# Inverses of a chunked recurrence on TensorE: the transposed half kept with exchanged partition halves, X and T products issued together

## The chip, the cores and the metric

One NeuronCore of one Trainium2 chip runs the whole kernel in a single launch. The metric is the time of one execution in device microseconds. Times of single instructions come from one profiled execution of the same program.

## The reference, cut to what matters

The reference is two transformer-like blocks over 256 tokens of width 1024, all in float32. The second block has a bidirectional recurrence with 8 heads of 64 columns:

```python
def step(S, inp):
    r_t, w_t, k_t, v_t, kk_t, a_t = inp
    s_kk = jnp.einsum('bhij,bhj->bhi', S, kk_t)
    S = (S * w_t[:, :, None, :]
         - s_kk[..., None] * (a_t * kk_t)[:, :, None, :]
         + v_t[..., None] * k_t[:, :, None, :])
    return S, jnp.einsum('bhij,bhj->bhi', S, r_t)
```

It runs once forward and once backward over the tokens. The kernel computes it in two chunks of 128 tokens. Inside a chunk the term with s_kk makes each token depend on those before it; written out for the chunk this is a triangular system, I + N, for each head and direction. So each chunk needs 16 inverses of 128x128 triangular matrices (8 heads, 2 directions). Ahead of the recurrence stand the first block and the projections, behind it banded attention, output projections and a mixture of 16 experts.

## The kernel before, in words

The kernel is one program in which each engine has its own instruction stream, and semaphores join them. PSUM has eight banks; for each bank two counters exist, `full[b]` (TensorE has finished a filling) and `evac[b]` (some engine has emptied it). The table STAGES lists how often each stage fills each bank; `take` lets PE wait until a bank is empty, `got` lets a reader wait until it is full, and `evacuated` waits until it has been emptied. A filling's place is given by its stage, its bank and its number in that stage.

The loop `for s in range(2)` goes over the two chunks. For each chunk:

- PE makes the score matrices (line 1427) and DVE copies their kept parts into AM (line 2833). ACT takes the two 64x64 diagonal blocks of each into AD (line 2106).
- PE makes the right-hand sides W (lines 1442 and 1446 for the first chunk, 1461 and 1467 for the second); ACT copies them out (line 2118).
- The inverse. The two 64x64 diagonal blocks of every matrix lie in the two partition halves (0 to 63 and 64 to 127). Xw holds the running inverse, XT its transpose, 8 heads in each direction d, 128x512 numbers for a direction. There are N_LEV = 6 levels. A level lv from 1 to 5 does: POOL makes the mask product NL of that level (line 908); PE makes P = NL times Xw (call at line 1493), ACT copies it into Pw (line 2122); PE makes two families, the X products from XT and Pw (call at line 1502) and the T products from Pw and XT (call at line 1504); DVE subtracts them from Xw and XT (line 2856). Level 0 is short: PE transposes NL with an identity (line 1485), DVE subtracts the result from the identity to get Xw (line 2844), and makes XT from NL itself (line 2840, with the semaphore x_init).
- All these products go through the helper `diagonal`, whose matmul is at line 1477. It reads and writes the same partition half, 16 matmuls of 64x64 with 64 columns for a direction. A matmul of float32 leaves two records in the trace, here called passes. P goes to banks 0 and 3, X to banks 1 and 5, T to banks 2 and 6 (direction 0 and 1).
- The blocks off the diagonal: line 1512 (AM and Xw, read out by ACT at line 2127), line 1523 (Pw and XT, read out by ACT at lines 2134 and 2136 into EB), then the inverse is put to W at lines 1534 and 1541, with the gate products (`gate2`, matmuls at line 927) between.

The order of work on PE is the written one: in a level P for direction 0, P for direction 1, then X and T for direction 0, then X and T for direction 1. Each waits with `take` for its bank and with `evacuated` for its operands. ACT takes its copies in the order of P, DVE its updates in the order Xw(0), XT(0), Xw(1), XT(1). SP's queue loads the weights: one part from a ring of four pages, the expert weights when counters such as `ex_started` say that PE has come far enough. No transfer belongs to the inverse.

Of the kernel before, what the change touches and what calls it, by code (L numbers as in the profile page):

```python
# [23 lines left out]
HEADS = 8  # L24
# [20 lines left out]
H = P // 2  # L45
# [43 lines left out]
for _s in range(2):  # L89
    STAGES += [(f"am{_s}", {0: 4, 1: 4, 2: 4, 3: 4}), (f"wv{_s}", {2: 1, 6: 1, **({3: 1, 7: 1} if _s else {})}),  # L90
               (f"inv{_s}", {0: 6, 3: 6, 1: 6, 5: 6, 2: 6, 6: 6}),
               (f"tail{_s}", {0: 1, 5: 1, 1: 1 - _s, 6: 1 - _s, 2: 1, 3: 1, 7: 2})]
# [50 lines left out]

LORA_BANKS = (7, 5, 6)
# [200 lines left out]
def build(nc, dram, out_dram):  # L345
# [8 lines left out]
    with ctx:  # L354
# [292 lines left out]
        x_init = sem("x_init")  # L647
# [195 lines left out]
        def _(pool):  # L843
# [45 lines left out]
            for s in range(2):  # L889
# [9 lines left out]
                for lv in range(1, N_LEV):  # L899
                    for d in range(2):  # L900
                        u8 = slice(8 * d, 8 * d + 8)
                        if lv == 1:

                            got(pool, f"inv{s}", (1, 5)[d], 0)
                            pool.wait_ge(x_init, 2 * s + d + 1)
                        else:
                            got(pool, f"inv{s}", 3 * d, lv - 2)
# [8 lines left out]
        def _(pe):  # L916
# [498 lines left out]
            for s in range(2):  # L1415
# [17 lines left out]
                if s == 0:  # L1433
                    evacuated(pe, "toks", 5, 2)
                    evacuated(pe, "toks", 6, 2)
                    for d in range(2):
                        take(pe, "wv0", 2 + 4 * d, 0)
                    for b in range(4):
                        evacuated(pe, "am0", b, 3)
                    for hd in range(HEADS):  # L1440
                        for d, near in enumerate((lo64, hi64)):
                            mm(ps[2 + 4 * d][near, 64 * hd:64 * hd + 64], lhsT=AM[near, 8 * d + hd, 256 + near.start:256 + near.stop],
                               rhs=Vtok[near, d, 64 * hd:64 * hd + 64], start=True, stop=True)
                    for hd in range(HEADS):
                        for d, far in enumerate((hi64, lo64)):
                            ins = mm(ps[2 + 4 * d][far, 64 * hd:64 * hd + 64], lhsT=AM[:, 8 * d + hd, 256 + far.start:256 + far.stop],
                                     rhs=Vtok[:, d, 64 * hd:64 * hd + 64], start=True, stop=True)
                            if hd == HEADS - 1:
                                ins.then_inc(full[2 + 4 * d], 1)
                else:  # L1450
                    for d in range(2):
                        evacuated(pe, "tail0", (1, 6)[d], 0)
                        for par in range(2):
                            take(pe, "wv1", 2 + 4 * d + par, 0)
                    for b in range(4):
                        evacuated(pe, "am1", b, 3)
                    for j in range(4):
                        for d in range(2):
                            for par in range(2):
                                hd = 2 * j + par  # L1460
                                mm(ps[2 + 4 * d + par][:, 64 * j:64 * j + 64], lhsT=AM[:, 8 * d + hd, 256:384],
                                   rhs=Vtok[:, 1 - d, 64 * hd:64 * hd + 64], start=True, stop=False)
                        for d in range(2):
                            row = 8 * d + 2 * j + 1 - d
                            for par, r64 in enumerate((lo64, hi64)):
                                b = 2 + 4 * d + par
# [5 lines left out]
                def diagonal(out, d, lhs, rhs):  # L1472

                    for hd in range(HEADS):
                        for q_ in range(2):
                            r64 = slice(H * q_, H * q_ + H)
                            ins = mm(out[r64, H * hd:H * hd + H], lhsT=lhs[r64, 8 * d + hd, :],  # L1477
                                     rhs=eye2[r64, :] if rhs is None else rhs[r64, 8 * d + hd, :], start=True, stop=True)
                    return ins

                for d in range(2):
# [3 lines left out]
                    diagonal(ps[bx], d, NL, None).then_inc(full[bx], 1)  # L1485
                for lv in range(1, N_LEV):
                    for d in range(2):
# [40 lines left out]
                for d in range(2):  # L1528
                    for b in (2 + 4 * d, 3 + 4 * d)[:1 + s]:
# [7 lines left out]
                for d in range(2):  # L1537
                    evacuated(pe, f"inv{s}", (2, 6)[d], 5)
# [261 lines left out]
        def _(act):  # L1800
# [296 lines left out]
            for s in range(2):  # L2097
# [10 lines left out]
                for d in range(2):  # L2108
                    if s:
                        got(act, "tail0", 2 + d, 0)  # L2110
                    for par in range(1 + s):
                        b = 2 + 4 * d + par
# [953 lines left out]
```

## Time and profile before

| what | value |
|---|---|
| median of three runs | 2027.17 us |
| lowest and highest | 2021.96, 2028.55 us |
| the profiled execution | 2026.23 us |
| its span, first to last instruction | 2024.3 us |
| mean granted TensorE clock | 0.943 |
| PE busy | 1784.4 us, 88% |
| DVE busy | 815.0 us, 40% |
| ACT busy | 307.4 us, 15% |
| POOL busy | 94.8 us, 5% |
| HBM read | 423.56 MB |

The profile gives for each engine the time in which it had an instruction in work; passes of TensorE overlap, so its busy time counts a stretch once however many run in it. The granted clock is a share of full speed: 1.00 is 2.4 GHz and 0.50 is 1.2 GHz. The chain that ended last goes back from the last instruction, each time to what released it. The page's slices show PE at 90% or more of the time until late in the run, and in the last part the DMA of the expert weights at some 430 GB/s.

### The profile page before, as it was taken

To read this page: it belongs to the slowest core of one execution; us is meant where nothing else is said; L and a number is where in the kernel's file an instruction comes from. 1 tells how busy PE (TensorE), PEld (TensorE's weight loads), DVE (VectorE), ACT (ScalarE), POOL (GpSimd) and SP (SyncE) were. 2 spreads that over 40 slices of the span, in tenths; PEclk is the share of its full clock that TensorE was granted. 3 is DMA by queue.
4 is the path that set the end of the run, shared out by engine and by line. 5 is a ranking of instruction groups with operands and counts; after the bars stand their busy time and mean duration, and the time that the engine had idled before them with its cause. 6 is when DMAs were issued, how large, how long until landed. Compare 5 with 4: busy or idle time off the path is not lost.

```text
span 2024.3 us, 29056 instructions
## 1 busy us (share of the span) xinstructions
PE 1784.4 (88%) x12002; PEld 1372.9 (68%) x12002; DVE 815.0 (40%) x1648; ACT 307.4 (15%) x704; POOL 94.8 (5%) x110
## 2 busy tenths in 40 slices
PE   7999999999999999999999998999997765565655
PEld 2788888888884877669999997878777221121212
DVE  3766666964431130734675247442534010000001
ACT  2200000011210111412111124222322000000000
POOL 2000000010100000000000002311001000000000
PEclk9999999999999999989999999999998877787887
DMA  8333335955441113116545852100467799999996
GB/s 356 127 131 142 126 128 181 350 202 187 146 146 62 63 63 125 63 63 229 186 166 188 291 189 102 44 23 24 145 253 308 331 433 428 433 435 427 432 435 255
DMA packets 46320, 426.10 MB, mean 210 GB/s; under 512 B 5283, under 2 KB 5764, under 8 KB 14988
## 3 DMA queue, kind: packets, MB, share of 16 engines
q1 hardware_dynamic: 36576, 387.04, 49.1%
q10 hardware_dynamic: 9644, 37.59, 5.2%
q8 instruction: 79, 1.29, 0.3%
q14 instruction: 21, 0.17, 0.0%
HBM read 423.56 MB, written 1.05 MB: 210 GB/s over the span
## 4 chain that ended last, share of the span: by engine, by line
PE 31%; DMA 19%; DVE 3%; issue 1%; POOL 1%; ACT 1%; SPq 0%; POOLq 0%; DVEq 0%; ACTq 0%
DMA arena<-experts_ring_dram 19%; PE bank L927 15%; PE bank L1102 6%; PE bank L1477 3%; PE bank L1726 2%; PE bank L1313 1%; DVE arena L2833 1%; PE bank L1580 0%; PE bank L1627 0%; POOL rstd L859 0%; PE bank L1363 0%; PE bank L1687 0%; DVE rstd L2234 0%; POOL arena L908 0%; PE bank L1646 0%
## 5 line engine op out<-in xcount | busy, mean ns | idle before, releaser
L927 PE MATMUL bank<-arena 128*128 128x256 f32 (+2 forms) x3552 | 684.8, 354 | 12.3 <-DVE arena L2739 5.6
L927 PEld LDWEIGHTS bank<-arena 128*128 128x128 f32 x3552 | 582.9, 192 | 104.8 <-issue 33.3
L1726 PE MATMUL bank<-arena 128*32 128x512 f32 x1536 | 237.9, 777 | 166.6 <-DMA arena<-experts_ring_dram 163.8
L1726 PEld LDWEIGHTS bank<-arena 128*32 128x32 f32 x1536 | 64.7, 137 | 334.1 <-issue 331.0
L1051 PE MATMUL bank<-arena 128*128 128x256 f32 x880 | 193.9, 379 | 0.0
L1051 PEld LDWEIGHTS bank<-arena 128*128 128x128 f32 x880 | 167.1, 190 | 23.1 <-issue 0.5
L1102 PE MATMUL bank<-arena 128*128 128x128 f32 x1064 | 119.0, 275 | 0.0
L1102 PEld LDWEIGHTS bank<-arena 128*128 128x128 f32 x1064 | 118.9, 192 | 0.0
L3026 DVE TENSOR_TENSOR arena<-arena,bank 128x512 f32<-128x512 f32 x8 | 5.5, 688 | 251.0 <-PE bank L1726 251.0
L2398 DVE SCALAR_TENSOR_TENSOR arena<-arena 128x1024 f32<-128x1024 f32 x56 | 68.3, 1220 | 0.0
L859 POOL TENSOR_TENSOR rstd<-sq 128x128 f32<-128x128 f32 (+2 forms) x9 | 6.6, 738 | 1258.5 <-ACT sq L1817 1258.5
L1477 PE MATMUL bank<-arena 64*64 64x64 f32 x2048 | 61.0, 218 | 1.1 <-POOL arena L908 1.0
L1477 PEld LDWEIGHTS bank<-arena 64*64 64x64 f32 x2048 | 60.2, 135 | 1.8 <-POOL arena L908 1.7
L3032 DVE COPY arena<-bank 128x512 f32<-128x512 f32 x4 | 2.8, 691 | 143.0 <-PE bank L1726 143.0
L1194 PE MATMUL bank<-arena 128*128 128x256 f32 x256 | 55.6, 379 | 0.0
L1817 ACT ACTIVATE sq<-bank 128x128 f32<-128x128 f32 (+1 forms) x48 | 14.9, 311 | 255.1 <-PE bank L927 224.0
L1194 PEld LDWEIGHTS bank<-arena 128*128 128x128 f32 x256 | 48.6, 190 | 7.0 <-issue 0.5
L2397 DVE SCALAR_TENSOR_TENSOR fh<-arena 128x1024 f32<-128x1024 f32 x36 | 44.0, 1224 | 13.7 <-DMA arena<-ada_rest_dram 11.4
L1313 PE MATMUL bank<-arena 128*128 128x128 f32 x384 | 47.2, 279 | 1.1 <-DVE arena L2266 1.0
L1313 PEld LDWEIGHTS bank<-arena 128*128 128x128 f32 x384 | 44.6, 192 | 3.1 <-DVE arena L2266 2.9
L1875 ACT ACTIVATE arena<-bank 128x256 f32<-128x256 f32 x22 | 8.3, 382 | 227.0 <-PE bank L1051 227.0
L1817 ACT ACTIVATE sq<-arena 128x128 f32<-128x128 f32 (+2 forms) x80 | 29.0, 371 | 86.3 <-DVE arena L2947 47.1
(399 smaller groups left out, 1845.0 us busy)
## 6 DMA issues: line engine op xcount, KB each, us to landing
arena<-dense_dram SPq DMA_DIRECT2D x167, 1024.0 KB, 4.8
arena<-experts_ring_dram SPq DMA_DIRECT2D x41, 4096.0 KB, 26.9
arena<-ada_rest_dram ACTq DMA_DIRECT2D x56, 512.0 KB, 5.3
arena<-experts_dram SPq DMA_DIRECT2D x21, 1024.0 KB, 9.3
arena<-ada_head_dram SPq DMA_DIRECT2D x8, 1024.0 KB, 23.8
arena<-experts_ring_dram SPq DMA_DIRECT2D x2, 2048.0 KB, 25.6
arena<-experts_dram SPq DMA_DIRECT2D x6, 512.0 KB, 11.5
arena<-tokens_dram ACTq DMA_DIRECT2D x1, 2048.0 KB, 20.8
```

Source lines behind the costliest of these rows:

```text
L927: ins = mm(out, lhsT=w, rhs=rhs(k), start=k == 0, stop=k == k_tiles - 1)
L1051: ins = mm(ps[b][:, o:o + T], lhsT=lhs(k), rhs=rhs(k), start=k == 0, stop=k == 3)
L1102: ins = mm(ps[b][:, o:o + P], lhsT=lhs(k), rhs=rhs(k), start=k == 0, stop=k == 3)
L1194: ins = mm(ps[tt][:, 0:256], lhsT=h1[:, k, tt * P:tt * P + P], rhs=ring_wide[slot][:, k, :], start=k == 0, stop=k == KD - 1)
L1313: ins = mm(ps[b][:, o:o + P], lhsT=w, rhs=h[:, k, half * P:half * P + P], start=k == 0, stop=k == KD - 1)
L1477: ins = mm(out[r64, H * hd:H * hd + H], lhsT=lhs[r64, 8 * d + hd, :], rhs=eye2[r64, :] if rhs is None else rhs[r64, 8 * d + hd, :], start= ...
L1726: ins = mm(ps[banks[half]][32 * e:32 * e + 32, :], lhsT=lhs[:, 2 * kp + par, CAP * e:CAP * e + CAP], rhs=slab[e][par][:, half * 512:half * ...
L1817: A(square_slot(r, j, n), src, ACT.Square).then_inc(ready, 1)
L1875: A(in_up[s][:, 0, :], ps[a][:, 0:T], ACT.Copy).then_inc(in_copied, 1)
L2397: stt(scratch[:, :], w, 1.0, cond_wide[:, 0:D], mult, mult, accum_out=ada_acc[:, 2 * t:2 * t + 1])
L2398: stt(w, w, 1.0, cond_wide[:, D:2 * D], mult, mult, accum_out=ada_acc[:, 2 * t + 1:2 * t + 2]).then_inc(ada_used, 1)
L2833: V.copy_predicated(AM[:, 8 * d + hd, :], keep_bits[:, d, :], ps[b][:, :]).then_inc(evac[b], 1)
```

## The change

XT is kept with its partition halves exchanged: what belongs to the upper block lies in partitions 0 to 63, and the other way round. Pw is made the same way, since P is now written to the other half. Then an X product reads one half and writes the other, and a T product reads and writes the exchanged half. PE issues them head by head: two X matmuls, two T matmuls, each of the four on another quarter of the array.

At level 0 XT no longer comes from NL by DVE. PE sends NL through the identity into exchanged halves (two matmuls with 512 columns for a direction, banks 2 and 6), and DVE subtracts that from the identity. POOL waits for this product, as it read NL, before it makes the next mask. The semaphore x_init is gone.

In the last level T has to return to its own halves. PE first sends XT through the identity into bank 2 or 6 (two matmuls with 512 columns), and the T products are added to it there, across halves, with Pw negated by ACT; DVE adds instead of subtracting for Xw, and ACT copies the bank to XT. The fillings of banks 2 and 6 become 7 a chunk, one more.

The right-hand sides W move from banks 2, 6, 3, 7 to 0, 3, 7, 6 (RIGHT_BANKS, at lines 1442 to 1467 and in ACT's copies at line 2118), as the level-0 transfer needs 2 and 6.

The diff, cut to its core (the renaming of W's banks is left out):

```diff
-    STAGES += [(f"am{_s}", {0: 4, 1: 4, 2: 4, 3: 4}), (f"wv{_s}", {2: 1, 6: 1, **({3: 1, 7: 1} if _s else {})}),
-               (f"inv{_s}", {0: 6, 3: 6, 1: 6, 5: 6, 2: 6, 6: 6}),
+    STAGES += [(f"am{_s}", {0: 4, 1: 4, 2: 4, 3: 4}), (f"wv{_s}", {0: 1, 3: 1, **({7: 1, 6: 1} if _s else {})}),
+               (f"inv{_s}", {0: 6, 3: 6, 1: 6, 5: 6, 2: 7, 6: 7}),
                (f"tail{_s}", {0: 1, 5: 1, 1: 1 - _s, 6: 1 - _s, 2: 1, 3: 1, 7: 2})]
...
 
...
                             got(pool, f"inv{s}", (1, 5)[d], 0)
-                            pool.wait_ge(x_init, 2 * s + d + 1)
+                            got(pool, f"inv{s}", (2, 6)[d], 0)
                         else:
                             got(pool, f"inv{s}", 3 * d, lv - 2)
                         nc.gpsimd.tensor_tensor(NL[:, u8, :], AD[:, u8, :],
...
-                def diagonal(out, d, lhs, rhs):
-
-                    for hd in range(HEADS):
-                        for q_ in range(2):
-                            r64 = slice(H * q_, H * q_ + H)
-                            ins = mm(out[r64, H * hd:H * hd + H], lhsT=lhs[r64, 8 * d + hd, :],
-                                     rhs=eye2[r64, :] if rhs is None else rhs[r64, 8 * d + hd, :], start=True, stop=True)
-                    return ins
+                halves = (lo64, hi64)
 
                 for d in range(2):
                     bx = (1, 5)[d]
                     pe.wait_ge(nl_ready, s * 2 * N_LEV + d + 1)
                     take(pe, f"inv{s}", bx, 0)
-                    diagonal(ps[bx], d, NL, None).then_inc(full[bx], 1)
+                    for hd in range(HEADS):
+                        for r64 in halves:
+                            ins = mm(ps[bx][r64, H * hd:H * hd + H], lhsT=NL[r64, 8 * d + hd, :], rhs=eye2[r64, :],
+                                     start=True, stop=True)
+                    ins.then_inc(full[bx], 1)
+                    bt = (2, 6)[d]
+                    take(pe, f"inv{s}", bt, 0)
+                    for q_, r64 in enumerate(halves):
+                        ins = mm(ps[bt][halves[1 - q_], :], lhsT=eye2[r64, :], rhs=NL[r64, 8 * d:8 * d + 8, :], start=True, stop=True)
+                    ins.then_inc(full[bt], 1)
                 for lv in range(1, N_LEV):
+                    last = lv == N_LEV - 1
                     for d in range(2):
                         b = 3 * d
                         pe.wait_ge(nl_ready, s * 2 * N_LEV + lv * 2 + d + 1)
 
                         evacuated(pe, f"inv{s}", (1, 5)[d], lv - 1)
                         take(pe, f"inv{s}", b, lv - 1)
-                        diagonal(ps[b], d, NL, Xw).then_inc(full[b], 1)
+                        for hd in range(HEADS):
+                            for q_, r64 in enumerate(halves):
+                                ins = mm(ps[b][halves[1 - q_], H * hd:H * hd + H], lhsT=NL[r64, 8 * d + hd, :],
+                                         rhs=Xw[r64, 8 * d + hd, :], start=True, stop=True)
+                        ins.then_inc(full[b], 1)
                     for d in range(2):
                         b, bx, bt = 3 * d, (1, 5)[d], (2, 6)[d]
+                        evacuated(pe, f"inv{s}", bt, lv - 1)
+                        take(pe, f"inv{s}", bx, lv)
+                        take(pe, f"inv{s}", bt, lv)
+                        if last:
+                            for q_, r64 in enumerate(halves):
+                                mm(ps[bt][r64, :], lhsT=eye2[halves[1 - q_], :], rhs=XT[halves[1 - q_], 8 * d:8 * d + 8, :],
+                                   start=True, stop=False)
                         evacuated(pe, f"inv{s}", b, lv - 1)
-                        if lv == 1:
-                            pe.wait_ge(x_init, 2 * s + d + 1)
-                        else:
-                            evacuated(pe, f"inv{s}", bt, lv - 2)
-                        take(pe, f"inv{s}", bx, lv)
-                        diagonal(ps[bx], d, XT, Pw).then_inc(full[bx], 1)
-                        take(pe, f"inv{s}", bt, lv - 1)
-                        diagonal(ps[bt], d, Pw, XT).then_inc(full[bt], 1)
+                        for hd in range(HEADS):
+                            c64 = slice(H * hd, H * hd + H)
+                            for q_, r64 in enumerate(halves):
+                                o64 = halves[1 - q_]
+                                ins = mm(ps[bx][r64, c64], lhsT=XT[o64, 8 * d + hd, :], rhs=Pw[o64, 8 * d + hd, :],
+                                         start=True, stop=True)
+                            if hd == HEADS - 1:
+                                ins.then_inc(full[bx], 1)
+                            for q_, r64 in enumerate(halves):
+                                o64 = halves[1 - q_]
+                                ins = mm(ps[bt][r64 if last else o64, c64], lhsT=Pw[o64, 8 * d + hd, :], rhs=XT[o64, 8 * d + hd, :],
+                                         start=not last, stop=not last or hd == HEADS - 1)
+                        ins.then_inc(full[bt], 1)
 
                 for d in range(2):
...
                 for d in range(2):
                     evacuated(pe, f"inv{s}", 3 * d, 5)
-                    evacuated(pe, f"inv{s}", (2, 6)[d], 4)
-                    take(pe, f"inv{s}", (2, 6)[d], 5)
+                    evacuated(pe, f"inv{s}", (2, 6)[d], 5)
+                    take(pe, f"inv{s}", (2, 6)[d], 6)
                 for hd in range(HEADS):
...
                     for d in range(2):
                         got(act, f"inv{s}", 3 * d, use)
-                        A(Pw[:, 8 * d:8 * d + 8, :], ps[3 * d][:, :].rearrange("p (i n) -> p i n", n=H), ACT.Copy)\
-                            .then_inc(evac[3 * d], 1)
+                        A(Pw[:, 8 * d:8 * d + 8, :], ps[3 * d][:, :].rearrange("p (i n) -> p i n", n=H), ACT.Copy,
+                          scale=1.0 if use < N_LEV - 2 else -1.0).then_inc(evac[3 * d], 1)
+                for d in range(2):
+                    bt = (2, 6)[d]
+                    got(act, f"inv{s}", bt, 5)
+                    A(XT[:, 8 * d:8 * d + 8, :], ps[bt][:, :].rearrange("p (i n) -> p i n", n=H), ACT.Copy).then_inc(evac[bt], 1)
                 for d in range(2):
                     far = (slice(H, P), slice(0, H))[d]
                     got(act, f"inv{s}", 3 * d, 5)
...
                         got(act, "tail0", 2 + d, 0)
-                    evacuated(act, f"inv{s}", (2, 6)[d], 4)
+                    evacuated(act, f"inv{s}", (2, 6)[d], 5)
                     A(EB[far, 8 * d:8 * d + 8, :], XT[far, 8 * d:8 * d + 8, :], ACT.Copy)
-                    got(act, f"inv{s}", (2, 6)[d], 5)
+                    got(act, f"inv{s}", (2, 6)[d], 6)
                     A(EB[near, 8 * d:8 * d + 8, :], ps[(2, 6)[d]][near, :].rearrange("p (i n) -> p i n", n=H), ACT.Copy,
...
                 eye8 = eye2.unsqueeze(1).to_broadcast([P, 8, H])
                 for d in range(2):
-                    dve.wait_ge(nl_ready, s * 2 * N_LEV + d + 1)
-                    if s:
-
-                        got(dve, "tail0", 2 + d, 0)
-                    tt_(XT[:, 8 * d:8 * d + 8, :], eye8, NL[:, 8 * d:8 * d + 8, :], sub).then_inc(x_init, 1)
-                for d in range(2):
-                    bx = (1, 5)[d]
-                    got(dve, f"inv{s}", bx, 0)
-                    tt_(Xw[:, 8 * d:8 * d + 8, :], eye8, ps[bx][:, :].rearrange("p (i n) -> p i n", n=H), sub)\
-                        .then_inc(evac[bx], 1)
+                    for dst, b in ((Xw, (1, 5)[d]), (XT, (2, 6)[d])):
+                        got(dve, f"inv{s}", b, 0)
+                        tt_(dst[:, 8 * d:8 * d + 8, :], eye8, ps[b][:, :].rearrange("p (i n) -> p i n", n=H), sub).then_inc(evac[b], 1)
                 for lv in range(1, N_LEV):
                     for d in range(2):
                         bx, bt = (1, 5)[d], (2, 6)[d]
                         evacuated(dve, f"inv{s}", bx, lv - 1)
-                        if lv == 1:
-                            dve.wait_ge(x_init, 2 * s + d + 1)
-                        else:
-                            evacuated(dve, f"inv{s}", bt, lv - 2)
-                        for dst, b, k in ((Xw[:, 8 * d:8 * d + 8, :], bx, lv), (XT[:, 8 * d:8 * d + 8, :], bt, lv - 1)):
-                            got(dve, f"inv{s}", b, k)
-                            tt_(dst, dst, ps[b][:, :].rearrange("p (i n) -> p i n", n=H), sub).then_inc(evac[b], 1)
+                        evacuated(dve, f"inv{s}", bt, lv - 1)
+                        for dst, b in ((Xw[:, 8 * d:8 * d + 8, :], bx), (XT[:, 8 * d:8 * d + 8, :], bt))[:1 if lv == N_LEV - 1 else 2]:
+                            got(dve, f"inv{s}", b, lv)
+                            tt_(dst, dst, ps[b][:, :].rearrange("p (i n) -> p i n", n=H), sub if lv < N_LEV - 1 else add)\
+                                .then_inc(evac[b], 1)
                 got(dve, f"tail{s}", 3, 0)
                 ts_(nU[1], ps[3][:, :].rearrange("p (h n) -> p h n", n=64), -1.0, None, mult).then_inc(evac[3], 1)
                 for d in range(2):
```

## Rows read from the trace of the kernel before

**Rows 1.** The page: the chain that ended last, by engine.
```profile
PE 31%; DMA 19%; DVE 3%; issue 1%; POOL 1%; ACT 1%; SPq 0%; POOLq 0%; DVEq 0%; ACTq 0%
```

**Rows 2.** The chain in order of time, both recurrences: start us, us, what.
```profile
1294.36 2.50 POOL arena L908 x2
...
1296.91 27.28 PE bank L1477 x928
...
1324.35 1.13 PE bank L1512 x31
...
1327.07 1.13 PE bank L1523 x31
...
1328.91 1.15 PE bank L1534 x32
1330.06 3.65 PE bank L927 x16
...
1365.39 27.28 PE bank L1477 x928
...
1395.54 1.55 PE bank L1523 x31
...
1397.91 1.98 PE bank L1534 x32
1399.88 5.13 PE bank L927 x16
```

**Rows 3.** The view of line 1477: durations (min/median/max ns), idle before it, who waited for it.
```profile
L1477 PE MATMUL bank<-arena x2048: 217/218/267, 1293.1 to 1392.5; 64*64 64x64 f32 x187
...
  POOL arena L908: 2.6, 6
...
  DVE arena L2856: 27.5, 20
```

**Rows 4.** Timeline of the first inverse: start us, us, engine, line, operation, [idle before it].
```profile
1293.12 2.08 PE L1477 MATMUL bank<-arena 64*64 64x64 f32 x64
...
1294.32 0.69 DVE L2844 TENSOR_TENSOR arena<-arena,bank 128x512 f32<-128x512 f32 x1
...
1295.68 16.49 PE L1477 MATMUL bank<-arena 64*64 64x64 f32 x548 [0.48 <-POOL arena L908]
...
1302.77 0.60 ACT L2122 ACTIVATE arena<-bank 128x512 f32<-128x512 f32 x1 [4.07 <-PE bank L1477]
...
1308.37 0.60 ACT L2122 ACTIVATE arena<-bank 128x512 f32<-128x512 f32 x1 [4.07 <-PE bank L1477]
```

**Rows 5.** Timeline of line 1541, two column halves of the array.
```profile
1333.74 0.22 PE L1541 MATMUL bank<-arena 128*64 128x64 f32 x1
1333.75 0.22 PE L1541 MATMUL bank<-fh,arena 128*64 128x64 f32 x1
1333.80 0.22 PE L1541 MATMUL bank<-arena 128*64 128x64 f32 x1
```

**Rows 6.** Tiled and untiled products: two timeline rows, one group (busy us, mean ns).
```profile
1279.69 2.00 PE L1427 MATMUL bank<-arena 64*128 64x256 f32 x16
...
1594.89 3.64 PE L1726 MATMUL bank<-arena 128*32 128x512 f32 x32 [2.80 <-DMA arena<-experts_dram]
...
L927 PE MATMUL bank<-arena 128*128 128x512 f32 x128 | 56.2, 592 | 0.0
```

**Rows 7.** Timeline: ten DVE operations of 128x512 in a row.
```profile
1284.61 6.20 DVE L2833 COPY_PREDICATED arena<-arena,bank 128x512 f32<-128x512 uint32 x10
```

**Rows 8.** Stretches behind the inverses: engines' busy us, then granted clock, DMA share, GB/s.
```profile
1324.00:1330.00 6.00, 3.58 (x105) 3.19 (x99) 0.78 (x2) 3.56 (x6) 0.00 (x0) 1.00 0.00 0
...
1395.00:1400.00 5.00, 3.69 (x65) 3.45 (x66) 0.00 (x0) 2.62 (x5) 0.00 (x0) 0.60 0.00 0
```

**Rows 9.** The chain as the expert products begin.
```profile
1574.78 11.29 PE bank L1726 x101
1586.09 18.37 DMA arena<-experts_ring_dram
```

More of the change, by code:

```diff
@@ L141, in gate2_at @@
     return (f"tail{t // 2}", 7, t % 2) if t < 4 else ("gates2", 2 + t % 2, t // 2 - 2)
+RIGHT_BANKS = ((0, 7), (3, 6))
 LORA_BANKS = (7, 5, 6)
@@ L646, in build @@
         am_zero = sem("am_zero")
-        x_init = sem("x_init")
         nl_ready = sem("nl_ready")
@@ L1436, in _ @@
                     for d in range(2):
-                        take(pe, "wv0", 2 + 4 * d, 0)
+                        take(pe, "wv0", RIGHT_BANKS[d][0], 0)
                     for b in range(4):
@@ L1441, in _ @@
                         for d, near in enumerate((lo64, hi64)):
-                            mm(ps[2 + 4 * d][near, 64 * hd:64 * hd + 64], lhsT=AM[near, 8 * d + hd, 256 + near.start:256 + near.stop],
+                            mm(ps[RIGHT_BANKS[d][0]][near, 64 * hd:64 * hd + 64], lhsT=AM[near, 8 * d + hd, 256 + near.start:256 + near.stop],
                                rhs=Vtok[near, d, 64 * hd:64 * hd + 64], start=True, stop=True)
@@ L1445, in _ @@
                         for d, far in enumerate((hi64, lo64)):
-                            ins = mm(ps[2 + 4 * d][far, 64 * hd:64 * hd + 64], lhsT=AM[:, 8 * d + hd, 256 + far.start:256 + far.stop],
+                            ins = mm(ps[RIGHT_BANKS[d][0]][far, 64 * hd:64 * hd + 64], lhsT=AM[:, 8 * d + hd, 256 + far.start:256 + far.stop],
                                      rhs=Vtok[:, d, 64 * hd:64 * hd + 64], start=True, stop=True)
                             if hd == HEADS - 1:
-                                ins.then_inc(full[2 + 4 * d], 1)
+                                ins.then_inc(full[RIGHT_BANKS[d][0]], 1)
                 else:
@@ L1453, in _ @@
                         for par in range(2):
-                            take(pe, "wv1", 2 + 4 * d + par, 0)
+                            take(pe, "wv1", RIGHT_BANKS[d][par], 0)
                     for b in range(4):
@@ L1460, in _ @@
                                 hd = 2 * j + par
-                                mm(ps[2 + 4 * d + par][:, 64 * j:64 * j + 64], lhsT=AM[:, 8 * d + hd, 256:384],
+                                mm(ps[RIGHT_BANKS[d][par]][:, 64 * j:64 * j + 64], lhsT=AM[:, 8 * d + hd, 256:384],
                                    rhs=Vtok[:, 1 - d, 64 * hd:64 * hd + 64], start=True, stop=False)
@@ L1465, in _ @@
                             for par, r64 in enumerate((lo64, hi64)):
-                                b = 2 + 4 * d + par
+                                b = RIGHT_BANKS[d][par]
                                 ins = mm(ps[b][:, 64 * j:64 * j + 64], lhsT=QQ[r64, 2 * row, :], rhs=state_v[r64, d, j, :],
@@ L1528, in _ @@
                 for d in range(2):
-                    for b in (2 + 4 * d, 3 + 4 * d)[:1 + s]:
+                    for b in RIGHT_BANKS[d][:1 + s]:
                         evacuated(pe, f"wv{s}", b, 0)
@@ L1537, in _ @@
                 for d in range(2):
-                    evacuated(pe, f"inv{s}", (2, 6)[d], 5)
+                    evacuated(pe, f"inv{s}", (2, 6)[d], 6)
                 for hd in range(HEADS):
@@ L2111, in _ @@
                     for par in range(1 + s):
-                        b = 2 + 4 * d + par
+                        b = RIGHT_BANKS[d][par]
                         got(act, f"wv{s}", b, 0)
```

## The prediction

> **What bounds the kernel now.** I read the page first. The chain that ended last runs through PE for 31% of the span and through DMA, that of the expert weights, for 19% [rows 1]. Such shares say nothing about one stage, so I went to the chain in order of time [rows 2]. The part that the change touches is the inverse of the first and of the second recurrence. Each stands in the chain as one unbroken piece of 27.28 us of line 1477 (the helper that issues all small products of the inverse), with POOL ahead of it (two steps, 2.50 us in the first), and behind it the closing products at lines 1512, 1523 and 1534. From the first product at 1293.12 [rows 4] to the closing one at 1324.35 the first inverse takes 31.23 us; the second has the same piece of 27.28 us, so I take it as equal. Together they are 62.5 us, 3.1% of the span: this is all that can change.
>
> The view of line 1477 [rows 3] says who waits for whom. PE lost 2.6 us there to POOL, and DVE lost 27.5 us waiting for PE. So PE bounds the levels, and its matmuls do. The source has 1024 products in that line and the trace 2048 records, two passes for a product. One level repeats every 5.60 us (ACT's copy at 1302.77 and again at 1308.37) and has 192 passes: 29.2 ns a pass, 0.93 us for the 32 passes of one family in one direction [rows 4].
>
> Is a pass 29 ns because PE issues no faster, or because only two of four quarters of the array work? Line 1541, which has two column halves, shows passes in pairs some 10 ns apart, and then 50 to 60 ns to the next pair [rows 5]. So a tile needs 58 ns for a pass of 64 columns, and the two tiles that work run side by side. The expert products show more: 32 passes of 512 columns in four column tiles take 3.64 us, 114 ns each, while 128 of the same width over the whole array take 56.2 us, 439 ns each [rows 6]. Four tiles at once are real on this chip. Row halves overlap too: line 1427 has 16 passes of 256 columns in 2.00 us, 125 ns each, where 16 passes on the full array, line 927, take 3.65 us, 228 ns each [rows 2, 6].
>
> **The change part by part.** The names: P is the product NL times Xw, X and T the two families that update Xw and XT, d the direction, 0 or 1.
>
> Moved: XT with its partition halves exchanged makes X read from one half and write to the other, while T stays on the diagonal. Issued head by head, X and T of one direction hold all four quarters. Today they take 2 x 0.93 = 1.87 us a direction. No row shows four 64x64 quarters together, so the bounds are 0.93 us (all four run like the pairs) and 1.87 us (two at a time). I take 0.93: both kinds of pair and a set of four column tiles overlap fully [rows 5, 6]. The Trainium skill, TensorE: Matmul & The Clock Gate, section "Wait — 56ns, not 53.3ns?", says that starts of matmuls never come closer than about 25 ns however small they are. The pairs above are closer singly, but no row here has a mean below it. By that rule the 64 passes would take 1.60 us, the period would be 5.15 us and the two recurrences would cost 4.3 us more instead of 3.4 less: 2031.5.
>
> Period of a level, with 0 at the end of X/T for direction 0. A result is there about 0.16 us after its slot (a pass lasts 218 ns and its slot 58) [rows 3]; DVE's start adds about 0.1 to 0.15, and X's last pass comes 0.06 before the end, so DVE starts Xw(0) at 0.25. Its operations follow each other at 0.61 us, since ten of 128x512 take 6.20 us [rows 7]: XT(0) at 0.86, Xw(1) at 1.50, done at 2.19 (0.69 each [rows 4]). PE meanwhile does X/T of direction 1 (to 0.93) and the next P(0) (to 1.98), and then, other than today, waits for Xw(1): P(1) runs from 2.30 to 3.25. X/T for direction 0 follows, to 4.2. ACT's copy of P(1) (0.21 + 0.60) ends at 4.06, in time. POOL's two masks, 2.50 us a level [rows 2], start behind P and stay hidden; so does DVE's XT(1), done at 2.8. So a level takes 4.2 us, not 5.60, and what is late next is DVE: three of its operations lie ahead of P(1). PE's gain of 1.87 us a level becomes 1.4.
>
> Added at the start: NL goes through the identity into exchanged halves, per direction two products of 512 columns in two quarters, two passes at 0.44 us [rows 6], 0.88 us. They replace DVE's first two XT operations at line 2840, which are off the path. POOL's next mask must wait for them. Today P(1) of the first level starts 3.79 us behind the first product. After: 0.05 to fill the array (64 passes take 2.08 us, the last result's 0.16 in it [rows 4]), 0.93, 0.88, 0.93, 0.88 make 3.67, or 3.23 where X(1) uses the quarters that the transfer of direction 0 leaves free; then 0.16, a hand-over of 0.10, POOL's 1.25 (half of 2.50) and one to PE of 0.05 (POOL ends at 1296.86, PE starts at 1296.91 [rows 2]): 5.23, or 4.79. So +1.0 to +1.5 us; I take +1.3.
>
> Added in the last level: T must come back to its own halves, so XT goes once more through the identity (0.88 us a direction) and T writes across like X. X and T then share two quarters: 1.87 us. The level ends with 2 x (0.88 + 1.87) = 5.5 us in place of 3.73. ACT copies XT out instead of DVE (two operations of 0.60 us, before its copy for line 1512's result, hidden by line 1512 itself). DVE's last Xw(1) can no longer hide behind T(1): 0.25 + 0.69 + 0.26 to PE's restart make 1.2 us, where today PE restarts 0.16 us behind the chain's last piece of line 1477 [rows 2].
>
> Banks for the right-hand sides, one wait fewer, a negated copy scale: nothing. The new banks 0, 3, 6 and 7 are emptied by ACT's copies of some 0.6 us while the first products run, well before P takes bank 0 at 1295.68, 2.56 us behind them [rows 4]; if that cover went, one copy of 0.6 us would show. The matching numbers of the semaphores cost nothing either.
>
> Sum for one recurrence, from P(1) of level 1 to line 1512. Today 1324.35 - 1296.91 = 27.44 us [rows 2]. After: P(1) 0.98 and X/T(0) 0.93 make 1.91; three periods 12.6; on to the end of the last P(1), 3.25; the last level's 5.5; 1.2. That is 24.46, so -2.98; with the start's +1.3, -1.7 us. Two recurrences: -3.4 us. Nothing behind catches it: the chain goes on through PE up to the expert products, and the expert loads that fill the tail are started by PE's progress [rows 9]. The profiled execution took 2026.23 us (span 2024.3), 0.05% under the median of 2027.17; against the median the sum gives 2023.8.
>
> **The rivals.** First, **the quarters do not add up** (slower). If two row halves and two column halves together cannot be fed or drained, X/T stays at 1.87 us: the period is 1.87 + 0.93 + 1.0 + 1.87 = 5.65, P(1) to line 1512 is 0.98 + 1.87 + 16.95 + 3.8 + 6.7 = 30.3, +2.9, and with the start +4.2 us; twice, +8.3: 2035.5. It turns from gain to loss where X/T is above some 1.35 us. The Trainium skill, TensorEngine Tiling (Array Packing), "Gotcha 1: PSUM Pressure", says that different row tiles cannot use one PSUM bank at the same time, which would give this time. The trace disagrees for two tiles: today's diagonal writes both row halves to one bank at 29 ns a pass. Chance 0.13.
>
> Second, **four quarters run, but are not fed fast enough**, by PE's sequencer or by the weight loads that go with each pass. Four passes in 58 ns are one in 15 ns, with a weight load each; the trace has bursts of neighbours 10 ns apart but no stretch with a mean below 29 [rows 5]. Half way between the bounds X/T is 1.40, the period 1.40 + 0.95 + 1.0 + 1.40 = 4.75, the total 0.98 + 1.40 + 14.25 + 3.35 + 6.7 = 26.7, so -0.75 and +1.3; twice +1.1: 2028.3. The Trainium skill's figure above lies beyond the middle. Chance 0.15.
>
> Third, **the clock** (faster). Behind the second inverse the granted clock falls to a mean of 0.60, which mixes 2.4 GHz with 1.2 GHz; behind the first it is 1.00, with the same waits for ACT ahead [rows 8]; lines 1523 and 1534 and a gate product take 1.55, 1.98 and 5.13 us there against 1.13, 1.15 and 3.65 [rows 2], 2.7 us more. If the shift takes that away: -6.1, 2021.1. If the first inverse gets it too, 2026.5, still inside the middle. Chance 0.12 for the gain.
>
> **How the numbers follow.** The forecast has 0.60: 2023.8 us, 0.17% below before, with its own range 2020 to 2028 (the bounds of the start, and runs of one kernel that lie 6.6 us apart). 0.3%, 6.1 us, is about what a measurement of this kernel can tell from no change. Faster by more: most of the third rival and a sixth of the forecast's scatter, 0.20. Slower by more: the first rival and a little of the second, 0.14. Within: 0.66. The range 2019 to 2033 takes in the second and third rivals and leaves the first outside.
>
> **What would show it.** Right: ACT's copies of one direction 4.2 us apart instead of 5.60; passes of X/T in fours within some 25 ns, 58 ns from four to four; PE waiting about 0.3 us a level for DVE's line of Xw; the inverse 29.5 us from first product to line 1512. Wrong: a period of 4.75 or 5.65 us (rivals two and one), PE without a gap in the levels, a granted clock below 1.00 between the first product and line 1512, or a first P(1) more than 5.5 us behind the first product.

## The result, and the profile after

The kernel after took 2033.88 us (median of 20 runs, 2028.48 to 2039.88), the kernel before 2026.71 in the same rounds (20 runs, 2019.75 to 2033.30): a ratio of 1.0036, 95% interval 1.0026 to 1.0047. The change made the kernel slower by 7 us. The forecast was 2023.8 with a range of 2019 to 2033: the range ended 0.9 us short, and the likeliest case had the wrong sign. The profiled execution after has a span of 2029.8 us. All ratios below are those on record with their 95% interval; they need not equal the quotient of the two medians.

The page of after, engines and chain. Against [rows 1] it shows nothing: a few microseconds do not move such shares.

```profile
PE 1776.7 (88%) x12034; PEld 1365.3 (67%) x12034; DVE 811.0 (40%) x1644; ACT 309.7 (15%) x708; POOL 94.9 (5%) x110
...
PE 31%; DMA 19%; DVE 3%; issue 1%; ACT 1%; POOL 1%; SPq 0%; POOLq 0%; DVEq 0%; ACTq 0%
```

Timeline of after, ACT, first inverse: its copies of P for direction 0 and 1 (start us, us, engine, line, operation). The line is that of the copies in [rows 4].

```profile
1289.47 0.60 ACT L2141 ACTIVATE arena<-bank 128x512 f32<-128x512 f32 x1 [3.33 <-PE bank L1498]
...
1293.71 0.60 ACT L2141 ACTIVATE arena<-bank 128x512 f32<-128x512 f32 x1 [2.42 <-PE bank L1498]
1294.90 0.60 ACT L2141 ACTIVATE arena<-bank 128x512 f32<-128x512 f32 x1 [0.60 <-PE bank L1498]
1299.39 0.60 ACT L2141 ACTIVATE arena<-bank 128x512 f32<-128x512 f32 x1 [3.89 <-PE bank L1498]
...
1304.47 0.60 ACT L2141 ACTIVATE arena<-bank 128x512 f32<-128x512 f32 x1 [3.35 <-PE bank L1498]
...
1311.35 0.60 ACT L2141 ACTIVATE arena<-bank 128x512 f32<-128x512 f32 x1 [3.89 <-PE bank L1498]
```

The first period is 4.24 us, as forecast. Then come 5.68, 5.08 and 6.88, where before had an even 5.60. One level ran as planned, and the next did not, with the same instructions. So the question is not what a level costs but what came in between. The chain of after in order of time answers it (start us, us, what):

```profile
1289.50 1.09 PE bank L1498 x30
...
1296.45 1.39 issue
1297.84 0.21 PE bank L1521
...
1301.07 0.70 issue
1301.77 0.27 PE bank L1521 x2
...
1304.78 1.00 issue
1305.78 0.98 PE bank L1498 x27
...
1308.31 1.37 issue
1309.68 0.27 PE bank L1515 x2
...
1312.43 0.86 PE bank L1508 x4
...
1315.16 0.86 PE bank L1508 x4
...
1317.92 0.70 DVE arena L2869
1318.62 0.25 issue
1318.87 1.13 PE bank L1531 x31
```

"Issue" is time in which PE waited for nothing that the profile shows. Four such pieces, 4.46 us together, lie in the middle of a family of products (lines 1515 and 1521 are X and T, 1498 is P). The waits of PE say the same, for the first inverse of after and then for that of before:

```profile
engine line waited for: us in total, times, longest us
PE bank L1521 <- issue: 2.1, 2, 1.4
PE bank L1515 <- issue: 1.4, 1, 1.4
PE bank L1498 <- issue: 1.0, 1, 1.0
PE bank L1531 <- DVE arena L2869: 1.0, 1, 1.0
PE bank L1498 <- POOL arena L908: 0.3, 1, 0.3
```

```profile
engine line waited for: us in total, times, longest us
PE bank L1477 <- POOL arena L908: 0.5, 1, 0.5
PE bank L1512 <- issue: 0.2, 1, 0.2
```

Counting the records between the restarts (the ends of these gaps) gives the key. From each restart to the next gap there are exactly 256 PE instructions: 252 matmuls and weight loads and 4 waits or register steps. And the instruction queue (q8 of the page), which moves blocks of 16 KB, shows one block ahead of each restart:

```
block starts   landed     PE restarts   PE instructions since the last restart
1295.49        1296.60    1297.84       -
1298.98        1300.27    1301.77       256
1303.00        1304.26    1305.78       256
1307.31        1308.24    1309.68       256
```

So PE ran out of instructions. The table also shows a round trip: a block starts 1.1 to 1.5 us behind a restart, takes 0.9 to 1.3 us to land, and PE restarts 1.2 to 1.5 us after that, 3.9 to 4.0 us in all. PE had used up the instructions of one restart in 2.3 to 3.0 us.

Before had the same blocks, one every 3.5 to 4.1 us (1299.77, 1303.54, 1307.16, 1310.63, 1314.71, 1318.67, 1322.59 in the first inverse), and needed them no faster: one of its levels is 388 PE instructions in 5.60 us, so 256 last it 3.7 us. It ran near the edge of the supply without showing it here.

From first product to closing line (1512, now 1531) the first inverse took 33.92 us (1284.95 to 1318.87) in place of 31.23, the second 36.76 in place of 31.24. Behind the second closing line no time changed: from there to the end of the profile it is 631.5 us in both kernels.

### The profile page after: what moved, and what is told of

Read it like the earlier page. It is cut to its first block, busy times and chain, and to the rows that moved or that the text cites. A ratio compares the mean times of both kernels' runs of the same rounds, so it can differ in the third digit from the quotient of the medians.

```text
span 2029.8 us, 29131 instructions
## 1 busy us (share of the span) xinstructions
PE 1776.7 (88%) x12034; PEld 1365.3 (67%) x12034; DVE 811.0 (40%) x1644; ACT 309.7 (15%) x708; POOL 94.9 (5%) x110
## 4 chain that ended last, share of the span: by engine, by line
PE 31%; DMA 19%; DVE 3%; issue 1%; ACT 1%; POOL 1%; SPq 0%; POOLq 0%; DVEq 0%; ACTq 0%
DMA arena<-experts_ring_dram 19%; PE bank L927 14%; PE bank L1102 6%; PE bank L1745 2%; PE bank L1313 1%; DVE arena L2856 1%; PE bank L1498 1%; PE bank L1515 1%; PE bank L1521 0%; PE bank L1599 0%; PE bank L1646 0%; POOL rstd L859 0%; PE bank L1363 0%; PE bank L1461 0%; DVE rstd L2257 0%
## 5 line engine op out<-in xcount | busy, mean ns | idle before, releaser
L1836 ACT ACTIVATE sq<-arena 128x128 f32<-128x128 f32 (+2 forms) x80 | 29.1, 371 | 86.5 <-DVE arena L2961 47.0
L1051 PE MATMUL bank<-fh,arena 128*128 128x256 f32 x176 | 41.6, 379 | 0.0
L2655 DVE TENSOR_REDUCE tiny<-bank 128x1 f32<-128x512 f32 x32 | 19.9, 682 | 53.2 <-PE bank L1232 53.2
```

Of the source, the lines that this page charges most:

```text
L1051: ins = mm(ps[b][:, o:o + T], lhsT=lhs(k), rhs=rhs(k), start=k == 0, stop=k == 3)
L1836: A(square_slot(r, j, n), src, ACT.Square).then_inc(ready, 1)
```

## The experiments

**The loop.** If the supply is short, PE must fetch less. Levels 1 to 4 of the changed kernel become a hardware loop on PE, whose body is fetched once. Four marker instructions a level, one ahead of each direction's P and one ahead of each direction's X and T, take the waits; otherwise the products are the same.

```diff
-                for lv in range(1, N_LEV):
-                    last = lv == N_LEV - 1
+                def level(lv, last=False):
...
+                        pe.sem_inc(pe_mark)
...
+                with pe.Fori(1, N_LEV - 1) as lv:
+                    level(lv)
+                level(N_LEV - 1, last=True)
```

> The changed kernel with PE's levels 1 to 4 in a hardware loop of four turns instead of written out (one body, 390 instructions; a counting instruction of the sequencer takes the waits on registers). Theory A, supply: straight code reaches PE in blocks of 256 instructions, one per some 3.9 us, and four quarters eat a block faster; in the loop only the first turn needs new blocks. Then levels 2 to 4 run without the gaps of 0.7 to 1.6 us, 4.2 to 4.5 us each instead of 5.6 to 5.9, which gives back 4 to 5 us per recurrence: 8 to 10 us less than the changed kernel, 1 to 3 us less than before. Theory B, the gaps come from four quarters at work (PSUM, weight loads, order of issue): the gaps stay in every turn and the time is that of the changed kernel, within 2 us.

Measured: 2025.02 us (12 runs) beside 2025.77 for before (29 runs), ratio 1.0001 (0.9985 to 1.0017). The loss is gone; the gain of 1 to 3 us over before that theory A added did not show. PE's waits in its first inverse, and the chain around a turn of the loop (1499 is P, 1517 X):

```profile
PE bank L1499 <- issue: 1.2, 4, 0.3
PE bank L1538 <- DVE arena L2876: 1.0, 1, 1.0
PE bank L1499 <- POOL arena L909: 0.6, 1, 0.6
```

```profile
1302.23 0.32 issue
1302.55 2.08 PE bank L1499 x64
...
1306.78 2.12 PE bank L1499 x64
```

ACT's copies are 4.90, 4.54, 4.57 and 4.23 us apart. The gaps in mid-family are gone; each turn of the loop costs 0.32 us in their place, and the last period, without a turn, is 4.23. No instruction block started between 1292.05, in the first turn, and 1308.79. A turn is 401 or 402 PE instructions in the trace and not the 390 expected: 384 matmuls and weight loads, the four markers, and 13 or 14 waits, register steps and a branch. The first inverse took 30.38 us.

**The control.** The same markers, levels written out.

```diff
-                with pe.Fori(1, N_LEV - 1) as lv:
+                for lv in range(1, N_LEV - 1):
```

> Control for the looped form of the changed kernel: the same two marker instructions a level that take the waits in the loop, but levels 1 to 4 written out as before. Theory (supply of instructions): without the loop the gaps after every 256 instructions are back, periods of 5.1 to 7.2 us, some 34 us from first product to closing line, and 2034 us. Rival (the markers, by taking the waits off the products, made the looped form fast): no gaps, periods of 4.2 us, and 2024 us.

Measured: 2034.40 us (12 runs), ratio 1.0053 (1.0034 to 1.0072). The waits and the chain of its first inverse have the gaps back, and ACT's copies are 4.25, 5.69, 4.87 and 7.08 us apart:

```profile
PE bank L1523 <- issue: 2.8, 2, 1.6
PE bank L1499 <- issue: 1.1, 1, 1.1
...
PE bank L1517 <- issue: 0.5, 1, 0.5
```

Three stretches of exactly 256 PE instructions lie between its restarts, which are 3.70, 3.66 and 4.48 us apart. So it is the loop, not the markers (four a level here too, not the two that the expectation names). The pair differs in the loop alone, in whether the products are fetched once or four times, and that is worth 9.4 us by the medians; the two ran in different rounds, and against before in its own rounds it is 0.52% or some 10.5 us.

**Before in a loop.** The same loop around levels 2 to 5 of the kernel before.

> The kernel before with PE's levels 2 to 5 in a hardware loop. Here two quarters work and 256 instructions take 3.74 us, so both theories expect no change but for the cost of the loop and of the waits moved to the sequencer: a level 5.6 to 5.8 us, the whole within 3 us of before. If it is faster by more, supply already held back the kernel before.

Measured: 2024.59 us (12 runs), ratio 0.9989 (0.9978 to 1.0001). Its levels are 5.99 to 6.02 us apart in the first inverse in place of 5.60, and the inverse takes 32.80 us. So in the profile the loop buys before nothing and costs it 0.4 us a level, as is to be expected where nothing starves. But the 1.5 us that the profile adds in the first inverse alone, 3 in two, do not appear in the time, and the interval, which ends at 0.2 us above before, leaves them out. The profile is of an execution of 2031.33 us, the longest of the twelve. This stays open.

**Two quarters at a time.** The change with all its moves, but X for all heads first, then T.

```diff
                            for q_, r64 in enumerate(halves):
...
+                        for hd in range(HEADS):
+                            c64 = slice(H * hd, H * hd + H)
+                            for q_, r64 in enumerate(halves):
...
```

> The changed kernel with X issued for all heads and then T for all heads, so that only two quarters work at a time; the instructions are the same in number. Theory A: a block of 256 takes 3.74 us of work then, about what supply gives, so the gaps vanish and the time stays that of the changed kernel within 3 us: levels of 5.65 us without gaps take the place of levels with gaps. If the four quarters brought what the prediction priced (0.93 us a direction and level), this would be 8 us slower than the changed kernel.

Measured: 2030.70 us (12 runs), ratio 1.0019 (1.0002 to 1.0035). PE's waits in its first inverse:

```profile
PE bank L1523 <- issue: 1.7, 3, 0.7
PE bank L1498 <- issue: 0.6, 1, 0.6
```

Theory A expected no gaps here, and missed. They are smaller (0.48 to 0.75 us in the chain, 2.4 us together) but still there, again after every 256 instructions, with only two quarters at work. So four quarters are not needed to stall PE. Nor did four save time over two as long as the levels are written out: this form is, if anything, the faster one (ratio 1.0019 against 1.0036, with intervals that overlap). It also says that the supply is not a constant: here the restarts are 4.07 to 4.24 us apart, where the first inverse of before, which never waited for one, had a block every 3.80 us on average in its first profile (1299.77 to 1322.59) and every 3.68 in its second. Why blocks came later here, no run shows.

**The rates by themselves.** A kernel that runs nothing but 64x64 products in fp32 from resident data, in sections; of the reference's computation it does nothing.

> A kernel that leaves out everything but PE products of 64x64 with 64 columns (its output is only some of the products). Sections in order: one quarter, two quarters and four quarters in straight code, four quarters in a loop of 8 turns, two quarters in a loop, four quarters straight again. Theory A: per pass 58 ns, 29 to 31 ns, 30 to 31 ns with a gap after every 256 instructions, 15 ns in the loop, 29 ns in the loop, and 30 to 31 ns again. Theory B: four quarters take the same per pass in straight code and in the loop.

Measured, per pass: one quarter 58.3 ns; two quarters written out 29.1, without a gap; four quarters written out 27.2, and 25.7 the second time, less than the 30 to 31 expected; two in a loop 29.1; four in a loop 16.6. The chain of the section with four quarters written out is a picture of starving:

```profile
92.84 1.36 issue
94.20 2.09 PE bank L36 x128
96.30 1.36 issue
97.66 2.09 PE bank L36 x128
99.75 1.36 issue
101.11 2.09 PE bank L36 x128
```

128 passes, 256 instructions, in 3.45 us: 13.5 ns an instruction. Most of the section's blocks take that long; some take 3.7 to 4.0. Two quarters written out need a block every 3.7 us, and there no gap shows. The two sections in a loop, four quarters and then two (engines' busy us and records, granted clock, DMA share, GB/s):

```profile
154.70:180.00 25.30, 23.58 (x1533) 22.89 (x1528) 0.00 (x0) 0.00 (x0) 1.00 0.01 1
180.30:224.80 44.50, 44.50 (x1532) 44.50 (x1530) 0.00 (x0) 0.00 (x0) 1.00 0.00 1
```

The same number of passes takes 25.3 and 44.5 us. The array and the sequencer can do four quarters; the supply of a written-out stream allows hardly more than two (27.2 and 25.7 against 29.1).

**Second profiles of both kernels.** One profile of each had left 5 us of the clock between them.

> The kernel before, unchanged, for a second profile. Both theories expect periods of 5.6 us from level 2 on and 31.2 us from the first product of an inverse to its closing line, wherever the blocks of instructions land. If the clock alone made the change slower (rival), this profile has no stretch of low clock between the first inverse and the second; if such a stretch is common to both kernels, it is here too, and the time from the closing line of the first inverse to the first product of the second is above the 16.6 us of the first profile by some 5 us.

> The kernel after, unchanged, for a second profile. Theory (supply of instructions): gaps of 0.7 to 1.6 us of PE again after every 256 of its instructions, with nothing waited for, and 33.9 us from first product to closing line in an inverse at full clock. Rival (clock): the gaps lie elsewhere or are gone, and the first inverse takes the 29.5 us of the forecast.

Measured: 2025.98 and 2032.31 us, one run each. Before: periods of 5.60 us in the first inverse, which takes 31.33 us. In the second inverse of this profile, against the expectation, before starves a little itself: ACT's copies at 1372.90, 1378.50, 1384.50 and 1390.39 are 5.60, 6.00 and 5.89 us apart, and PE starts no product for 0.33 us at 1382.87, for 0.28 at 1386.90 and for 0.14 at 1390.84, with exactly 256 of its instructions from one restart to the next. So the edge is there in the kernel before too. After: gaps after 256 instructions again, periods of 4.24, 5.92, 5.08 and 7.15 us, and 34.42 us. A stretch of low clock lies between the inverses in both kernels, as a row of the second profile of before and then one of the first profile of after show:

```profile
1351.00:1358.00 7.00, 7.00 (x39) 6.53 (x40) 0.95 (x2) 1.06 (x2) 1.26 (x1) 0.51 0.00 0
```

```profile
1355.00:1363.00 8.00, 8.00 (x68) 7.41 (x68) 0.00 (x0) 1.21 (x4) 0.00 (x0) 0.50 0.01 2
```

The first profile of before had none there, as its own row from one inverse to the next shows:

```profile
1325.00:1361.00 36.00, 32.28 (x394) 26.96 (x390) 14.04 (x23) 7.50 (x13) 2.54 (x2) 1.00 0.09 31
```

From the closing line of the first inverse to the first product of the second, that profile took 37.2 us (not the 16.6 that the expectation names), the first of after 42.7, and the second ones 45.1 (before) and 45.4 (after). And the first inverse, at a granted clock of 1.00 in all four, is 2.7 and 3.1 us longer in after. So the clock is no cause of the loss. Both inverses together, with the slow piece at the start of the second where there is one:

```
before             62.5, 64.2 us       loop + VectorE's order    61.5
after              70.7, 69.9          the same + split level    60.4, 60.6
markers only       70.5                loop around before        67.7
two quarters       69.5                loop around after         63.0
```

After less before is 8.2 us in the first pair of profiles and 5.7 in the second, 7.0 in the mean; the medians differ by 7.2. The slow piece at the start of the second inverse differs from profile to profile, so it is in part luck that the mean comes so close. From the second closing line to the end the second pair agrees as well, 628.8 us in before and 629.0 in after.

**Better forms.** First VectorE's updates in the order Xw(0), Xw(1), XT(0), XT(1), with the loop; then also a last level with both X first, then identity and T of each direction.

```diff
-                    for d in range(2):
-                        bx, bt = (1, 5)[d], (2, 6)[d]
...
+                    for half, banks in ((Xw, (1, 5)), (XT, (2, 6)))[:1 if lv == N_LEV - 1 else 2]:
+                        for d, b in enumerate(banks):
```

> The looped form of the changed kernel, and VectorE's updates put in the order Xw(0), Xw(1), XT(0), XT(1). Theory (once the supply is gone, a level is bound by the chain of products, copies and updates, and XT(0) need not wait behind both halves of the first direction): a level of 3.9 us with 0.3 us for the loop, so 4.2 in place of 4.55, about 1 us less in an inverse and 2 in all: 2023. Rival (VectorE's order is covered by PE's pairs): the levels stay at 4.55 and the time at 2025.

> As the run before, and the last level split: both X products first, then identity and T of each direction, so that VectorE's last update lies beside T. Theory: 0.9 us less in an inverse than the run before, 2 in all: 2021, faster than the kernel before by 0.2 to 0.3%. Rival (the time is set by something after the inverses, such as the loads of the following stage or the clock): the inverse ends 0.9 us sooner in the profile and the time stays at that of the run before.

> The best form again (loop, VectorE's order, split last level), for a second set of rounds. Theory: 0.1 to 0.3% below the kernel before again, 2021 to 2024 us, with 4.5 us a level from level 2 on. Rival (the first set was luck): a ratio of 1.000.

Measured: the order alone 2025.49 us, ratio 1.0003 (0.9985 to 1.0020); with the split level 2021.57 us, 0.9986 (0.9971 to 1.0000), and 2022.85, 0.9993 (0.9977 to 1.0009) in the second set, 12 runs each. The order bought nothing. The two copies of one level are now 0.93 us apart in place of 1.19, but the looped form had that already without the order. That fits the turn's 0.32 us in front of P covering DVE's lateness. The split level did what it should, 6.21 us from the last level's copy to the closing line in place of 7.27:

```profile
1310.43 2.08 PE bank L1499 x64
1312.51 1.93 PE bank L1533 x64
1315.30 0.93 PE bank L1546 x32
1317.09 0.93 PE bank L1546 x32
1318.02 0.95 PE bank L1560 x32
```

Line 1560, the closing one, follows the last T in the same breath (the chain of after has 1.07 us there). The best form is some 0.1% below before in two sets, and no single interval excludes no change. It is clearly below after.

## Why the prediction was wrong

**Right.** X and T of one direction on four quarters: the forecast was 0.93 us, and in the one level that was fed the 64 passes take 0.98 us (1290.38 to 1291.36), 15 ns each, in fours whose starts lie within 20 ns. These two groups of after in that stretch, X and T of direction 0, are busy side by side (busy us, mean ns):

```profile
L1521 PE MATMUL bank<-arena 64*64 64x64 f32 x32 | 1.1, 221 | 0.0
L1515 PE MATMUL bank<-arena 64*64 64x64 f32 x31 | 1.1, 218 | 0.0
```

The Trainium skill, TensorE: Matmul & The Clock Gate, section "Wait — 56ns, not 53.3ns?", has a floor of about 25 ns between starts; these 15 ns and the 16.6 of the loop above contradict it for products in different quarters. The 2031.5 us that the prediction worked out from it are near the measured time by luck: the cause is another. The Trainium skill, TensorEngine Tiling (Array Packing), "Gotcha 1: PSUM Pressure", says that different row tiles cannot use one PSUM bank at the same time. The same rows disagree, and with them the first rival: the X passes of both row halves go to one bank while all four quarters start a pass every 15 ns.

The period of a level was right too: forecast 4.2, measured 4.24 once in after and 4.23 in the last period of the looped form. PE's wait for DVE was forecast at 0.3 us a level and is 0.26 (copies 1.19 apart where 0.93 would be back to back). The last level's products were forecast at 5.5 us and take 5.37 (1312.43 to 1317.80), the restart behind them at 1.2 and takes 1.07. The start was put too high: P(1) stands 4.55 us behind the first product (1284.95 to 1289.50), 0.76 more than before and not 1.3. The level-0 products of direction 1 do use the quarters that the identity transfer leaves free (both run from 1286.19 on), and what P(1) waited for was not the last transfer but POOL's two masks, one behind the other from 1286.95 to 1289.44.

**The step that failed** is the one that multiplied a right period by the levels, "three periods 12.6". The four periods between ACT's copies took 21.88 us, where at 4.2 they are 16.8. Of these 5.1 us too many the chain's four pieces of "issue" are 4.46. The start, the last level and the restart behind it gave 0.8 us back against the forecast, so that the first inverse missed its 29.5 by 4.4. The forecast priced the array, the four engines and the hand-overs, and put the stream of instructions that feeds PE at nothing. The trace of before has its blocks, but at the pace of its own need and with no wait for them: it shows a supply that sufficed, and not by how little.

The second rival asked the right question ("not fed fast enough, by PE's sequencer or by the weight loads") and named the wrong feeder. The sequencer and the weight loads both pass the test of the loop: 16.6 ns a pass. As the feeder is neither, its price, a uniformly slower X/T at 2028.3 us, was wrong as well. Starving is not a slower rate but an account: 256 instructions come every 3.9 to 4.0 us here (the restarts above), though PE is through with them in 2.3 to 3.0. After needs 5.9 us less for four periods (16.8 in place of 22.69) and gets 0.8 of it. On top it pays 0.76 at the start and 2.7 from the last level's copy to the closing line (7.52 in place of 4.78), which no saving covers now: together the 2.7 us by which its first inverse is longer. The Trainium skill, Runtime: NRT & Kernel Launch, section "Instruction fetch mechanics", says that blocks hold 256 instructions, which the trace bears out to the instruction, and that the crossing is mostly hidden, which holds for the first profile of before and not for after.

**What hung on the clock** (third rival) did not come: the stretches of low clock around the inverses lie elsewhere from profile to profile of the same kernel, and in both kernels.

The step about the sum's basis failed in a small way: the second inverse was taken as equal to the first. In most profiles it is 1 to 3 us longer, and in these its first products still run at 1.2 GHz; in the second profile of before the small gaps above add some 0.7 us.

**Open.** What sets the pace of the supply: alone a block took 3.45 us at best, in this kernel the restarts are some 3.5 to 4.5 apart, and no run varied what else is fetched or moved. Why its blocks come later in some stretches and forms than in others (two quarters at a time, the second inverse in the second profile of before). And why the loop around before costs 3 us in the profile and none in the time.

## What to carry to other kernels

Where PE's products are small (here 64x64 in two passes, each with its weight load), count instructions as well as columns: a written-out stream that starved was fed 256 instructions per 3.5 to 4.5 us here, and before any change that packs more products into the same time the stretch's 256-blocks belong in the sum. A loop whose body is fetched once lifted that limit for 0.3 us a turn (0.4 in the kernel before). In a profile, "issue" in the middle of a family of equal products, at equal counts of instructions, is the sign; and a kernel that shows none may still be at the edge.

## What the runs showed of the hardware that was not expected

Four 64x64 quarters of the array, two row halves and two column halves, run fully side by side in fp32, at 15 to 17 ns a pass, weight loads included, where one quarter alone takes 58.3. PE's instructions come in blocks of 256, to a starving PE at best one in 3.45 us (13.5 ns an instruction). A loop body of 401 PE instructions, 384 of them matmuls and weight loads, ran on after its first turn without a fetch, at 0.32 us a turn. And around the two inverses stretches of 1.2 GHz of 3 to 17 us appear in some profiles and not in others of one kernel: one profile of each kernel would have put 5 us of clock on the change.
